# Idle transposes of the identity on TensorE, at five places of a decoder trunk's opening

## The chip, the cores and the metric

The kernel runs on one NeuronCore of a Trainium2 chip. The metric is the device time of one execution in microseconds; lower is better. The engines are TensorE (PE in the rows, its weight loads PEld), VectorE (DVE), ScalarE (ACT), GpSimd (POOL) and SyncE (SP), which issues most of the transfers.

## The reference

One inference step of a two-layer decoder trunk, in float32. A prompt of 512 tokens and 8 x 8 sample tokens go through the same weights: 576 tokens, model width 1024, feed-forward width 2816. Each layer is a half feed-forward, a mixer (a Conformer convolution in the first layer, dilated window attention in the second) and another half feed-forward. Cut to what matters here:

```python
def rmsnorm(x, g):
    xf = x.astype(jnp.float32)
    y = xf * lax.rsqrt(jnp.mean(xf * xf, axis=-1, keepdims=True) + EPS)
    return (y * g.astype(jnp.float32)).astype(x.dtype)

def swiglu_ffn(h, w_in, w_out):
    gate, up = jnp.split(h @ w_in, 2, axis=-1)
    return (jax.nn.silu(gate) * up) @ w_out

# for each layer li
x = x + 0.5 * swiglu_ffn(rmsnorm(x, norms[li, 0]), ffn_w_in[li, 0], ffn_w_out[li, 0])
...
```

The change touches only what runs ahead of and inside the first product of the first feed-forward.

## The kernel before

x is held transposed: model width on the partitions (eight tiles k of 128), tokens along the free side (576). x arrives in token order, in two halves of the columns (semaphores x_in0 and x_in1), as xr. TensorE turns each tile k with four transposes of 128 x 128 against the identity `ident` (L2361), and for every second k the 64 sample tokens of two tiles (L2369). Ahead of these it turns the six norm gains, loaded as rows of parR, with eight narrow transposes (L2349). ScalarE copies the turned tiles k = 0, 1, 2, 3, 6, 7 from PSUM to xT (L1209); VectorE copies 4 and 5 (L1762) and the sample parts (L1748).

A matmul of the feed-forward is not done as one product. Every float32 operand is split into a high part, cast by ScalarE to the type fp32r, and a low part, which VectorE gets by subtraction; a product is three matmuls, high by high, high by low, low by high (L2157 to L2159, 288 columns each). On top of this, the product of the first weight matrix with h is cut into 2 x 2 blocks (gate and up by the two halves of every pair of k tiles; the two halves of the tokens) and done with seven block products, P1 to P7, in place of eight. Their operands are sums of blocks:

- on the side of x, the terms: ScalarE multiplies xT by the gain (L1065, into hW and hM), VectorE forms sums (L1529 to L1535), ScalarE casts (L1071) and VectorE forms the low parts (L1542), into tE (for P1, P6, P5) and tM (for P2, P7, P3, P4). This is done for four pairs p of k tiles, one after the other;
- on the side of the weights: blk holds a unit's blocks as loaded (L614) and their sums (L1572, L1578, L1584). ScalarE casts (L1087) and VectorE forms the low parts (L1549), into hlA (A1 for P1, A2 for P2 and P4) and hlS (SA for P6 and P7, SB for P5 and P3).

The width 2816 is processed in two segments of eleven units of 128. `units` runs each unit's seven products, `outputs` the second weight matrix. The first unit of the first segment is `first_unit`: since its terms come out pair by pair, it runs the products' quarters by pair, P1, P6, P2, P7, P5 for p = 0, then for 1 and 2, then P4 and P3 for the three, then all seven for p = 3. Behind it stand two matmuls of the reciprocal norm's diagonal (L2258), then the second unit, which begins with P1 and needs its own A1.

Every engine has its own hand-written order and waits on semaphores: f_ready (weight parts), t_ready (terms), x_ready (tiles of xT), gain_ready (VectorE has copied the gains from PSUM bank 7). On ScalarE the order of the opening is: x tiles 0 and 1, the terms of pair 0, x tiles 2 and 3, casts of pair 0, x tiles 6 and 7, cast A1, the terms of pair 1, squares of x for the norm (L1197), cast SA, casts of pair 1, casts A2 and SB, and so on. On VectorE the order follows it.

Of the kernel before, what the change touches and what calls it, by code (L numbers as in the profile page):

```python
# [14 lines left out]
P = 128  # L15
# [111 lines left out]
def split_no(n, g, what, u):  # L127
    if n == g == u == 0 and what in FIRST_SPLITS:
        return FIRST_SPLITS.index(what) + 1
    return (SEGS * n + g) * len(SPLIT[g]) + SPLIT[g][what, u]  # L130
# [14 lines left out]
def term_no(n, p, x):  # L145


    base = 3 * (KD // 2) * n
    if n == 2:
        return base + (2 * p + x if x < 3 else KD + p + 1)  # L150
    return base + 3 * p + x
# [136 lines left out]
def trunk_program(nc, I, O):  # L288
# [3 lines left out]
    def place(name, shape, dt=f32):  # L292
        t = nc.alloc_sbuf_tensor_at(name, shape, dt, offset=at[0])
        at[0] += (int(np.prod(shape[1:])) * 4 + 31) // 32 * 32
        return t
# [10 lines left out]
    ident = place("ident", [P, P])  # L306
# [145 lines left out]
    ps = nc.alloc_psum_tensor("ps", [P, 8, 512], f32)  # L452
# [44 lines left out]
    S = {n: nc.alloc_semaphore(n) for n in names}  # L497
# [485 lines left out]
    def _(act):  # L983
# [391 lines left out]
        def keys_prompt(j, g):  # L1375

            q, _, _ = TURN["kp", j, g]
            act.wait_ge(S["t_mm"], q + 1)
            nc.scalar.copy(kT[:, j % 2, 4 * g:4 * g + 4, :].rearrange("p x n -> p (x n)"), turned(("kp", j, g))
                           ).then_inc(S["t_act"], 1)  # L1380

        def keys_sample(e, x, j):

            q, _, _ = TURN["ks", e, x, j]
            a = (C1, C2)[x]
            act.wait_ge(S["t_mm"], q + 1)
            nc.scalar.copy(kTs[:, j, a:a + 512], turned(("ks", e, x, j))).then_inc(S["t_act"], 1)
# [22 lines left out]
        for s in range(-1, UNITS + 3):  # L1410
            if 0 <= s - 1 < UNITS:
                exp(s - 1)
            ks = sample_keys_of(s)
            if ks and ks[1] < 2:
                for j in (0, 1, 3):
                    keys_sample(*ks, j)
            elif ks:
                keys_dense(ks[0])
            kp = prompt_keys_of(s)
            if kp:  # L1420
                keys_prompt(*kp)
            if 0 <= s - 2 < UNITS:
                q, _, _ = TURN["p", s - 2, 1]
                act.wait_ge(S["t_mm"], q + 1)
                nc.scalar.copy(pT[:, 4:8, :].rearrange("p x n -> p (x n)"), turned(("p", s - 2, 1))
                               ).then_inc(S["t_act"], 1)
# [669 lines left out]
    def _(pe):  # L2096
# [17 lines left out]
        def square_sum_tokens(bank=6):  # L2114
            t_ = tokens(tb)
            for t in range(TT):
                r = P if t < 4 else SMP
                nc.tensor.matmul(ps[0:r, bank, t:t + 1], t_[:, t * P:t * P + r], ones[:, 0:1], start=True, stop=True)
            return nc.tensor.matmul(ps[SMP:P, bank, 4:TT], t_[:, SEQ:TOK], ones[:, 0:1], start=True, stop=True)
# [32 lines left out]
        def quarter(what, p):  # L2152

            out = ps[:, P_BANK[what], 0:HALF]
            wh, wl = WEIGHTS[what]
            cols = slice(p * P, (p + 1) * P)
            nc.tensor.matmul(out, wh[:, cols], TERM[what][:, p, 0], start=p == 0, stop=False)  # L2157
            nc.tensor.matmul(out, wh[:, cols], TERM[what][:, p, 1], start=False, stop=False)  # L2158
            nx = nc.tensor.matmul(out, wl[:, cols], TERM[what][:, p, 0], start=False, stop=p == KD // 2 - 1)  # L2159
            if p == KD // 2 - 1:  # L2160
                nx.then_inc(S["f_mm"], 1)
# [6 lines left out]
        def parameters():  # L2168
            pe.wait_ge(S["par_in"], 16 * 9)
            for k in range(KD):  # L2170
                nx = nc.tensor.transpose(ps[:, 4, k * NPAR:(k + 1) * NPAR], parR[:, k * P:(k + 1) * P],
                                         ident[0:NPAR, 0:NPAR])
            nx.then_inc(S["par_t"], 1)

        def add_square(k):

            n, t = SQ["ffn3_in"] - 1, tokens((tb, ta)[k % 2])
            pe.wait_ge(S["sq_in"], KD * n + k + 1)
            for g, (a, b) in enumerate(((0, TOK - 2 * P), (2 * P, TOK))):
                nx = nc.tensor.matmul(ps[32 * g:32 * g + 32, 4, 0:b - a], ones[:, 0:32], t[:, a:b], start=k == 0,  # L2180
                                      stop=k == KD - 1, tile_position=(0, 32 * g))
            if k < KD - 2:
                nx.then_inc(S["sq_added"], 1)
            elif k == KD - 1:
                nx.then_inc(S["sq_ready"], 1)

        def turn_sums():

            a = HALF + SMP // 2
            pe.wait_ge(S["row_out"], 1)  # L2190
            for t in range(TT):
                g, c = divmod(t, 2) if t < 4 else (1, 2)
                rows, one = sum_rows[:, c * P:min(c * P + P, TOK - 2 * P)], ident[0:64, 32 * g:32 * g + 1]
                r = rows.shape[1]
                nc.tensor.matmul(ps[0:r, 4, a + t:a + t + 1], rows, one, start=True, stop=True)
            nx = nc.tensor.matmul(ps[SMP:P, 4, a + 4:a + 5], rows, one, start=True, stop=True)
            nx.then_inc(S["ss_done"], 1)

        def first_unit(n):

            x = KD * XV[f"ffn{n}_in"]

            def part(what, p):
                if p == 0:
                    pe.wait_ge(S["f_ready"], split_no(n, 0, {"P1": "A1", "P2": "A2", "P4": "A2", "P6": "SA", "P7": "SA",
                                                             "P5": "SB", "P3": "SB"}[what], 0))
                pe.wait_ge(S["t_ready"], term_no(n, p, {"P1": 1, "P5": 1, "P6": 2}.get(what, 3)))
                quarter(what, p)

            if n == 2:  # L2210

                for what in ("P1", "P6", "P5"):
                    if what == "P5":
                        pe.wait_ge(S["kv_evac"], 32)
                    for p in range(4):
                        part(what, p)
                pe.wait_ge(S["kv_evac"], 35)
                for p in range(4):
                    for what in ("P2", "P7", "P4", "P3"):
                        part(what, p)  # L2220
            else:
                if n == 0:
                    pe.wait_ge(S["x_ready"], KD)
                    pe.wait_ge(S["gain_ready"], 1)

                for p in range(3):
                    for what in ("P1", "P6", "P2"):
                        part(what, p)
                    if p == 0:
                        pe.wait_ge(S["x_ready"], x + KD - 1)  # L2230
                    for what in ("P7", "P5"):
                        part(what, p)
                if n == 3:
                    add_square(KD - 2)
                    add_square(KD - 1)
                elif n == 0:
                    parameters()
                pe.wait_ge(S["x_ready"], x + KD)
                if n == 1:
                    for p in range(3):  # L2240
                        part("P4", p)
                    pe.wait_ge(S["sq_ready"], SQ["ffn1_in"])
                    square_sum_tokens(4).then_inc(S["ss_done"], 1)
                    for p in range(3):
                        part("P3", p)
                else:
                    for p in range(3):
                        for what in ("P4", "P3"):
                            part(what, p)
                if n == 3:  # L2250
                    turn_sums()
                for what in FIRST[0]:
                    part(what, 3)

            pe.wait_ge(S["diag_ready"], n + 1)
            if n == 0:
                pe.wait_ge(S["par_ready"], 1)
            nc.tensor.matmul(ps[:, 4, :], ones[:], diag[:, 0:4].rearrange("p a b -> p (a b)"), start=True, stop=True  # L2258
                             ).then_inc(S["bc_mm"], 1)
# [84 lines left out]
        pe.wait_ge(S["ident_ready"], 1)  # L2344
        pe.wait_ge(S["consts_ready"], 1)

        pe.wait_ge(S["norms_in"], 16)
        for k in range(KD):
            nx = nc.tensor.transpose(ps[:, 7, k * 6:(k + 1) * 6], parR[NORM:NORM + 6, k * P:(k + 1) * P],  # L2349
                                     ident[0:6, 0:6])  # L2350
        nx.then_inc(S["gain_t"], 1)

        for k in range(KD):
            if k % 4 == 0:
# [489 lines left out]
```

## Time and profile before

| | us |
|---|---|
| median of 3 runs | 2262.54 |
| lowest and highest run | 2262.34, 2266.04 |
| the profiled execution | 2262.11 |
| its span, first to last instruction | 2260.2 |

| engine | busy us | share |
|---|---|---|
| TensorE, matmuls | 2214.9 | 98% |
| TensorE, weight loads | 2102.0 | 93% |
| VectorE | 1617.6 | 72% |
| ScalarE | 890.1 | 39% |
| GpSimd | 137.3 | 6% |

The span is cut on the page into 40 slices of 56.5 us, so the whole stretch that the change touches lies in the first. A timeline is needed for it: each of its rows gives the start, the length from the first start to the last end of the instructions that it merges, the engine, the line, what is written from what, and in brackets how long the engine sat idle before, and what let it go. A matmul's end is modelled, and matmuls overlap, so the spacing of starts says what one costs. The granted clock is 1.00 at 2.4 GHz and 0.50 at 1.2 GHz.

### The profile page before, as it was taken

What the parts mean: (1) busy time and instruction counts of PE and PEld (TensorE: products, weight loads), DVE (VectorE), ACT (ScalarE), POOL (GpSimd) and SP (SyncE); (2) the same over time, 40 slices, a digit from 0 to 9 for tenths busy, and PEclk for the clock granted to TensorE, in tenths of its full rate; (3) what the DMA queues carried; (4) which work ended last, traced back from release to release, by engine and by line L of the source; (5) the groups of instructions that cost most, each with busy time, mean ns of one, the idle gap of its engine ahead of it and who ended that gap; (6) DMA issues with size and microseconds to landing.
All of it is one profiled execution on the core that took longest, in us unless ns stands there. A gap on an engine that the chain in (4) does not pass through costs nothing.

```text
span 2260.2 us, 41620 instructions
## 1 busy us (share of the span) xinstructions
PE 2214.9 (98%) x17636; PEld 2102.0 (93%) x17636; DVE 1617.6 (72%) x2138; ACT 890.1 (39%) x1167; POOL 137.3 (6%) x191
## 2 busy tenths in 40 slices
PE   7999999999999999999999999999999999999998
PEld 6999999987799999998889999999987789999998
DVE  7983995699789849953358956984445479947963
ACT  6431443222654314432234422442145555413442
POOL 0000000323010000001001000001001100000001
PEclk8999999999899999999999999999999999999999
DMA  5543443554244435423439533532959933233321
GB/s 156 158 151 110 151 156 93 164 141 126 72 147 150 140 100 164 153 83 90 132 107 304 173 114 99 168 115 73 240 148 281 253 113 94 75 98 96 88 77 55
DMA packets 372091, 305.61 MB, mean 135 GB/s; under 512 B 13798, under 2 KB 338414, under 8 KB 371050
## 3 DMA queue, kind: packets, MB, share of 16 engines
q1 hardware_dynamic: 365485, 232.06, 36.4%
q0 software_dynamic: 6464, 71.76, 9.2%
q8 instruction: 86, 1.41, 0.3%
q14 instruction: 44, 0.35, 0.1%
q10 hardware_dynamic: 12, 0.02, 0.0%
HBM read 284.45 MB, written 70.54 MB: 157 GB/s over the span
## 4 chain that ended last, share of the span: by engine, by line
PE 88%; DVE 6%; issue 2%; ACT 2%; DMA 2%; SPq 1%; DVEq 0%; ACTq 0%
PE ps L2101 34%; PE ps L2157 13%; PE ps L2159 13%; PE ps L2158 13%; PE ps L2565 2%; PE ps L2563 2%; PE ps L2564 2%; PE ps L2401 2%; PE ps L2609 1%; DMA kc<-in_cache_kv_w 1%; DVE blk L1572 1%; PE ps L2725 1%; DVE hlS L1549 1%; PE ps L2663 1%; PE ps L2716 1%
## 5 line engine op out<-in xcount | busy, mean ns | idle before, releaser
L1087 ACT CAST hlS<-blk 128x1024 fp32r<-128x1024 f32 x176 | 184.3, 1053 | 207.0 <-PE ps L2159 169.4
L2101 PE MATMUL ps<-actH,oWA 128*128 128x288 f32 x1408 | 250.4, 296 | 0.0
L2101 PE MATMUL ps<-actH,oWB 128*128 128x288 f32 x1408 | 250.0, 296 | 0.0
L1716 DVE SCALAR_TENSOR_TENSOR cs<-ps,rstd 128x576 f32<-128x576 f32 x64 | 48.5, 757 | 246.9 <-PE ps L2101 246.9
L1549 DVE TENSOR_TENSOR hlS<-blk,hlS 128x1024 fp32r<-128x1024 f32 x176 | 213.5, 1216 | 2.4 <-ACT hlS L1087 2.4
L2157 PE MATMUL ps<-tM,hlA 128*128 128x288 f32 x704 | 212.4, 302 | 2.9 <-DVE hlA L1549 2.4
L2157 PE MATMUL ps<-tE,hlS 128*128 128x288 f32 x704 | 208.5, 296 | 4.1 <-DVE hlS L1549 4.1
L2101 PEld LDWEIGHTS ps<-actH,oWA 128*128 128x128 f32 x1408 | 209.0, 189 | 1.2 <-DVE cs L1611 0.6
L2101 PEld LDWEIGHTS ps<-actH,oWB 128*128 128x128 f32 x1408 | 209.0, 189 | 0.0
L2157 PE MATMUL ps<-tM,hlS 128*128 128x288 f32 x704 | 208.2, 296 | 0.0
L2158 PE MATMUL ps<-tM,hlA 128*128 128x288 f32 x704 | 208.0, 295 | 0.0
L2159 PE MATMUL ps<-tM,hlA 128*128 128x288 f32 x704 | 207.5, 295 | 0.0
L2158 PE MATMUL ps<-tE,hlS 128*128 128x288 f32 x704 | 207.5, 295 | 0.0
L2159 PE MATMUL ps<-tE,hlS 128*128 128x288 f32 x704 | 207.2, 294 | 0.0
L2158 PE MATMUL ps<-tM,hlS 128*128 128x288 f32 x704 | 207.2, 294 | 0.0
L2159 PE MATMUL ps<-tM,hlS 128*128 128x288 f32 x704 | 206.9, 294 | 0.0
L1488 DVE TENSOR_TENSOR wHL<-wst,wHL 128x1024 fp32r<-128x1024 f32 x64 | 82.2, 1285 | 116.8 <-ACT wHL L995 116.7
L1116 ACT ACTIVATE ta<-ta 128x576 f32<-128x576 f32 x88 | 60.5, 687 | 266.5 <-DVE ta L1631 266.5
L2101 PE MATMUL ps<-hH,wHL 128*128 128x288 f32 x896 | 158.5, 297 | 0.0
L1549 DVE TENSOR_TENSOR hlA<-blk,hlA 128x1536 fp32r<-128x1536 f32 (+2 forms) x104 | 156.0, 1504 | 0.9 <-ACT hlA L1087 0.9
L1087 ACT CAST hlA<-blk 128x1536 fp32r<-128x1536 f32 (+2 forms) x104 | 132.3, 1280 | 47.6 <-PE ps L2101 29.7
L2101 PE MATMUL ps<-actL,oWA 128*128 128x288 f32 x704 | 150.8, 296 | 0.0
(323 smaller groups left out, 5363.3 us busy)
## 6 DMA issues: line engine op xcount, KB each, us to landing
blk<-in_ffn_w_in SPq DMA_DIRECT2D x352, 256.0 KB, 4.1
raws<-in_ffn_w_out SPq DMA_DIRECT2D x64, 704.0 KB, 4.7
out_kv_sample<-in_cache_kv_w POOLq DMA_DIRECT2D x8, 4064.0 KB, 16.8
out_kv_sample<-in_cache_kv_w POOLq DMA_DIRECT2D x8, 2016.0 KB, 9.2
wst<-in_conv_w_pw SPq DMA_DIRECT2D x24, 512.0 KB, 4.1
wst<-in_w_kv SPq DMA_DIRECT2D x24, 512.0 KB, 3.8
kc<-in_cache_kv_w SPq DMA_DIRECT2D x40, 256.0 KB, 9.1
kc<-in_cache_kv_w SPq DMA_DIRECT2D x8, 1024.0 KB, 7.7
```

Source lines behind the costliest of these rows:

```text
L1087: nc.scalar.copy(o, a).then_inc(S["f_h"], 1)
L1116: nc.scalar.activation(ta[:], ta[:], ACT.Silu).then_inc(S["silu_done"], 1)
L1488: nc.vector.tensor_tensor(wL[:, s % 2, 0:size], wst[:, s, 0:size], wH[:, s % 2, 0:size].bitcast(f32), ALU.subtract).then_inc(S["w_ready"], 1)
L1549: nc.vector.tensor_tensor(o, a, h.bitcast(f32), ALU.subtract).then_inc(S["f_ready"], 1)
L1716: nc.vector.scalar_tensor_tensor(px[m % 2], pair(2 + m % 2), 0.5, rstd[:], ALU.mult, ALU.mult).then_inc(S["px_ready"], 1)
L2101: nx = nc.tensor.matmul(outs[t], a, b[:, t, :], start=start and first, stop=stop and b is xh and not first)
L2157: nc.tensor.matmul(out, wh[:, cols], TERM[what][:, p, 0], start=p == 0, stop=False)
L2158: nc.tensor.matmul(out, wh[:, cols], TERM[what][:, p, 1], start=False, stop=False)
L2159: nx = nc.tensor.matmul(out, wl[:, cols], TERM[what][:, p, 0], start=False, stop=p == KD // 2 - 1)
L2401: nc.tensor.matmul(ps[32 * g:32 * g + 32, 0, :], dW[:, s, g, k, :], uV[:, s, g, 4 * k:4 * k + SEQ], start=k == 0, stop=k == NS - 1, tile_p ...
L2563: nc.tensor.matmul(ps[:, t, :], xh, a, start=k == 0, stop=False)
L2564: nc.tensor.matmul(ps[:, t, :], xh, b, start=False, stop=False)
```

## The change

A helper, `keep_busy(bank, times)`, issues so many transposes of the identity by the identity, 128 x 128, into a PSUM bank that nothing reads before it is written anew. No semaphore is raised by them. It is called at five points of TensorE's program: 4 before the wait for the norms, 14 behind the gains' transposes, 28 before the first product (where the wait for gain_ready is now taken ahead of them, and the one for x_ready behind), 30 behind P1 of the first pair and 16 behind its P6; 92 in all. Only the first feed-forward (n = 0) is touched.

```diff
@@ -2196,6 +2196,11 @@
             nx = nc.tensor.matmul(ps[SMP:P, 4, a + 4:a + 5], rows, one, start=True, stop=True)
             nx.then_inc(S["ss_done"], 1)
 
+        def keep_busy(bank, times):
+
+            for _ in range(times):
+                nc.tensor.transpose(ps[:, bank, 0:P], ident[:], ident[:])
+
         def first_unit(n):
 
             x = KD * XV[f"ffn{n}_in"]
@@ -2220,12 +2225,15 @@
                         part(what, p)
             else:
                 if n == 0:
+                    pe.wait_ge(S["gain_ready"], 1)
+                    keep_busy(7, 28)
                     pe.wait_ge(S["x_ready"], KD)
-                    pe.wait_ge(S["gain_ready"], 1)
 
                 for p in range(3):
                     for what in ("P1", "P6", "P2"):
                         part(what, p)
+                        if n == p == 0 and what != "P2":
+                            keep_busy(4, 30 if what == "P1" else 16)
                     if p == 0:
                         pe.wait_ge(S["x_ready"], x + KD - 1)
                     for what in ("P7", "P5"):
@@ -2344,11 +2352,13 @@
         pe.wait_ge(S["ident_ready"], 1)
         pe.wait_ge(S["consts_ready"], 1)
 
+        keep_busy(6, 4)
         pe.wait_ge(S["norms_in"], 16)
         for k in range(KD):
             nx = nc.tensor.transpose(ps[:, 7, k * 6:(k + 1) * 6], parR[NORM:NORM + 6, k * P:(k + 1) * P],
                                      ident[0:6, 0:6])
         nx.then_inc(S["gain_t"], 1)
+        keep_busy(6, 14)
 
         for k in range(KD):
             if k % 4 == 0:
```

What the order of TensorE's instructions is at the beginning of the program: `ident` is the identity, `parR` the gains' rows, `xr` x in token order. Before:

```order
L2349 MATMUL ps<-ident,parR 128x6 x8
L2361 MATMUL ps<-ident,xr 128x128 x8
L2369 MATMUL ps<-ident,xr 128x64 x2
L2361 MATMUL ps<-ident,xr 128x128 x8
L2369 MATMUL ps<-ident,xr 128x64 x2
```

And with the change:

```order
L2202 MATMUL ps<-ident 128x128 x4
L2358 MATMUL ps<-ident,parR 128x6 x8
L2202 MATMUL ps<-ident 128x128 x14
L2371 MATMUL ps<-ident,xr 128x128 x8
L2379 MATMUL ps<-ident,xr 128x64 x2
L2371 MATMUL ps<-ident,xr 128x128 x8
```

Four idle transposes stand ahead of the gains' and fourteen between them and x; the rest keeps its order.

The same engine from the last tiles of x to P2 of the first pair, where tE and tM are the terms, hlA and hlS the weights. Before:

```order
L2361 MATMUL ps<-ident,xr 128x128 x8
L2369 MATMUL ps<-ident,xr 128x64 x2
L2157 MATMUL ps<-tE,hlA 128x288
L2158 MATMUL ps<-tE,hlA 128x288
L2159 MATMUL ps<-tE,hlA 128x288
L2157 MATMUL ps<-tE,hlS 128x288
L2158 MATMUL ps<-tE,hlS 128x288
L2159 MATMUL ps<-tE,hlS 128x288
L2157 MATMUL ps<-tM,hlA 128x288
```

And with the change:

```order
L2371 MATMUL ps<-ident,xr 128x128 x8
L2379 MATMUL ps<-ident,xr 128x64 x2
L2202 MATMUL ps<-ident 128x128 x28
L2157 MATMUL ps<-tE,hlA 128x288
L2158 MATMUL ps<-tE,hlA 128x288
L2159 MATMUL ps<-tE,hlA 128x288
L2202 MATMUL ps<-ident 128x128 x30
L2157 MATMUL ps<-tE,hlS 128x288
L2158 MATMUL ps<-tE,hlS 128x288
L2159 MATMUL ps<-tE,hlS 128x288
L2202 MATMUL ps<-ident 128x128 x16
L2157 MATMUL ps<-tM,hlA 128x288
```

Twenty-eight stand ahead of P1, thirty between P1 and P6, sixteen between P6 and P2. The orders of the other engines are the same before and after.

## Rows read from the trace of the kernel before

**Rows 1.** The page: span, and granted clock in 40 slices, in tenths.
```profile
span 2260.2 us, 41620 instructions
...
PEclk8999999999899999999999999999999999999999
```

**Rows 2.** Stretches (us): length, TensorE busy (matmuls), clock, DMA share, GB/s.
```profile
17.00:18.00 1.00, 0.36 (x1) 0.60 0.73 159
18.00:26.00 8.00, 1.79 (x6) 0.50 0.46 119
80.00:100.00 20.00, 20.00 (x152) 1.00 0.85 279
```

**Rows 3.** TensorE's timeline: start us, length us, line, operands, count, [idle before].
```profile
2.78 0.99 PE L2349 MATMUL ps<-ident,parR 6*128 6x6 f32 x8 [2.78 <-DMA parR<-in_norms]
6.91 1.97 PE L2361 MATMUL ps<-ident,xr 128*128 128x128 f32 x8 [3.14 <-DMA xr<-in_x_sample]
...
9.21 1.64 PE L2361 MATMUL ps<-ident,xr 128*128 128x128 f32 x8
...
11.04 1.09 PE L2361 MATMUL ps<-ident,xr 128*128 128x128 f32 x8
...
13.54 0.33 PE L2369 MATMUL ps<-ident,xr 64*128 64x64 f32 x2
17.64 0.58 PE L2157 MATMUL ps<-tE,hlA 128*128 128x288 f32 x1 [3.77 <-DVE hlA L1549]
...
22.83 0.61 PE L2157 MATMUL ps<-tE,hlS 128*128 128x288 f32 x1 [4.13 <-DVE hlS L1549]
...
26.27 0.61 PE L2157 MATMUL ps<-tM,hlA 128*128 128x288 f32 x1 [2.36 <-DVE hlA L1549]
...
30.76 0.34 PE L2157 MATMUL ps<-tM,hlS 128*128 128x288 f32 x1
...
40.82 0.40 PE L2157 MATMUL ps<-tE,hlA 128*128 128x288 f32 x1 [0.20 <-DVE hlA L1549]
```

**Rows 4.** Weight loads in 9.2 to 10 and 11 to 12: busy us, mean ns.
```profile
L2361 PEld LDWEIGHTS ps<-ident,xr 128*128 128x128 f32 x5 | 0.9, 218 | 0.1
...
L2361 PEld LDWEIGHTS ps<-ident,xr 128*128 128x128 f32 x8 | 0.9, 140 | 0.1
```

**Rows 5.** Timeline of the other engines, up to the first weight cast.
```profile
1.19 0.29 POOL L863 TENSOR_SCALAR_AFFINE_SELECT ident<-ident 128x128 f32<-128x128 f32 x1 [0.25 <-POOL ident L861]
...
8.06 0.58 ACT L1209 COPY xT<-ps 128x512 f32<-128x512 f32 x1 [5.20 <-PE ps L2361]
...
8.91 0.58 ACT L1209 COPY xT<-ps 128x512 f32<-128x512 f32 x1 [0.27 <-PE ps L2361]
...
9.63 0.29 DVE L1748 COPY xT<-ps 128x128 f32<-128x128 f32 x1 [5.62 <-ACT xT L1209]
10.02 0.78 ACT L1065 ACTIVATE hW<-xT,par 128x576 f32<-128x576 f32 x1 [0.53 <-DVE xT L1748]
...
15.23 0.64 ACT L1087 CAST hlA<-blk 128x512 fp32r<-128x512 f32 x1
```

**Rows 6.** The chain of waits: start us, length us, who.
```profile
16.79 0.60 DVE hlA L1549
...
40.09 0.68 DVE hlA L1549
```

**Rows 7.** TensorE's waits, 60 to 100 us: total, times, longest.
```profile
PE ps L2157 <- DVE hlA L1549: 0.9, 1, 0.9
```

**Rows 8.** x_sample's two transfers; the first unit's last two weight transfers: issue, landing.
```profile
L583 SPq DMA_DIRECT2D xr<-in_x_sample x2: 534/562/590, 1.3 to 2.5; - x2
...
DMA to landing us min/median/max: 5.6/6.8/8.0
...
L614 SPq DMA_DIRECT2D blk<-in_ffn_w_in x2: 1400/1640/1881, 4.3 to 5.7; - x2
...
DMA to landing us min/median/max: 8.2/8.4/8.7
```

## The prediction

> **What bounds the kernel now.** I read the page first, then the granted clock by stretches, then TensorE's own timeline of the first 41 us, and last the chain of waits over the same stretch, because the change touches nothing behind the first part of the opening unit.
>
> The page's clock row has an 8 only in the first of 40 slices [rows 1]. The change acts on that slice. The stretches show the clock at half level (0.50, 1.2 GHz) from 18 to 26 us, having fallen within the microsecond before [rows 2]. TensorE's timeline shows why there was little work [rows 3]: its last transpose of x starts at 13.54, the first product P1 waits 3.77 us until 17.64, P6 waits 4.13 until 22.83, and P2 waits 2.36 until 26.27. After that it runs without a wait, at first at 0.24 us a matmul (19 of them from 26.27 to 30.76 [rows 3]); at the full clock, from 80 to 100 us, 152 matmuls fill 20.00 us, 0.13 each [rows 2]. So 25 matmuls ran slowly, six of them in the first two products.
>
> There is a second slow piece, which the clock column doesn't show, since it reads 1.00 from the start. The first eight transposes of x took 1.97 us, the next eight 1.64, and eight of the same shape from 11.04 on 1.09 [rows 3]; weight loads of one shape fell from 218 to 140 ns in the mean [rows 4]. With the modelled end of one taken off (0.43 and 0.28 us), the spacing is (1.97 - 0.43)/7 = 0.22 and (1.09 - 0.28)/7 = 0.116 us, a factor of about two. I read this as half level at 6.91 and full level from some 10.2 on, and nothing but transposes ran between.
>
> Which of the two pieces sets the end? The chain of waits does not go through TensorE between 9 and 41 us. It leaves it after the first transposes of x (ScalarE copies at 8.06 and 8.91, VectorE's copy at 9.63, ScalarE's gain multiply at 10.02 [rows 5]) and then runs on VectorE and ScalarE alone, through the first hlA at 16.79, up to the hlA of the next unit at 40.09 [rows 6]. TensorE starts the next unit at 40.82, 0.20 us behind its own last work, let go by that hlA [rows 3]. It waits once more for 0.9 us between 60 and 100 us [rows 7], and the chain passes to it there. So what TensorE does faster between 17 and 40 us is absorbed at 40.82; what the first two groups of x do faster goes through.
>
> **The change part by part.** Base: the profiled execution took 2262.1 us, of which the span is 2260.2 and 1.9 lie around it; the median of the runs is 2262.5. I forecast differences and put them on the median.
>
> (1) Four transposes before the norms arrive. The identity is finished at 1.19 + 0.29 = 1.48 [rows 5]. At the slow spacing, 4 x 0.22 = 0.9 us, so the slot is free at about 2.5, before the norms' transposes at 2.78. Cost 0.
>
> (2) Fourteen more before x. The norms' eight transposes start at 2.78 and take 0.99 with the last one's end. 14 x 0.22 = 3.1 us from 3.6 ends at 6.7, just under the 6.91 at which x is there. Cost 0; if the first starts 0.3 later, 0.1 to 0.2 us. VectorE's copy of the gains depends only on what is ahead of these fourteen.
>
> (3) The transposes of x at full speed. The clock rose, before, some 3.4 us behind the start of the x transposes, and at 30.8, 4.6 us after the unbroken run began at 26.27 [rows 3]. Now TensorE works, almost unbroken, from 2.78. The two bounds put the rise at 6.2 to 7.4, where the transposes of x begin. At full speed the fourth transpose ends at 6.91 + 3 x 0.116 + 0.28 = 7.54 and the eighth at 8.00, against 8.0 and 8.88. ScalarE's first copy moves from 8.06 to 7.6; the second follows it on its engine at 8.15 instead of 8.91, since now ScalarE and not TensorE is late. VectorE's copy at 9.63 and all that hangs on it move by the same 0.76 us. The bounds for this term are 0 (the clock rises no sooner than before) and 0.8; I take 0.7. What could eat it next? The second half of x is all issued by 2.51 and lands within 8.0 us, thus by 10.5 [rows 8]; its transposes start at 11.04 before and can start at 10.5, soon enough for VectorE, which asks for them around 12. The last of the opening unit's four weight transfers lands at about 5.7 + 8.2 = 13.9 [rows 8]; the cast that needs it stands at 15.23 and would move to 14.5 [rows 5]. Neither takes the gain.
>
> (4) Twenty-eight before P1. They start when the last x tile is turned, 13.9 before and about 13.1 now: 28 x 0.116 = 3.25 us, end by 16.4, ready for P1 at 17.64 - 0.76 = 16.9. Cover about 0.5 us. Cost 0.
>
> (5) Thirty before P6: from about 17.3, 30 x 0.116 = 3.5, end 20.8 to 21.1, needed at 22.83 - 0.76 = 22.1. Cover 1.0 us, cost 0. Sixteen before P2: from 22.5, 16 x 0.116 = 1.9, end 24.4 to 24.7, needed at 25.5. Cost 0. No other queue is passed: the other engines' orders are unchanged.
>
> (6) The opening products at full speed. The gaps left are about 1 us, against 3.8 and 4.1, so the clock stays up. 25 matmuls x (0.24 - 0.13) = 2.7 us less TensorE work. TensorE then catches up with VectorE's terms of the third and fourth pair and waits for them. Its next unit still starts when VectorE has hlA. Value at the end: 0 by the chain, 2.7 as the far bound.
>
> Sum: 0 + 0 - 0.7 + 0 + 0 + 0 = -0.7 us, so 2262.5 - 0.7 = 2261.8.
>
> The row that the sum leans on is that transposes alone brought the clock up [rows 3, 4]. The Trainium skill, in "TensorE: Matmul & The Clock Gate", section "Part 4: PE-mode transpose", states the opposite: the full clock does not engage for transpose mode, since it doesn't count as TensorE being busy in the same way. By that rule the change would give the slower rival below; the trace of this case speaks against it.
>
> **Rivals.**
> *Slower: idle transposes at half level.* If the idle transposes don't raise or hold the clock, each block runs at 0.22. 28 x 0.22 = 6.2 from 13.9 puts P1 at about 20.1. 30 x 0.22 = 6.6 behind P1's 0.7 puts P6 at 27.4, and 16 x 0.22 = 3.5 behind its 0.7 puts P2 at 31.6, against 26.27. That is 5.3 us later, less the 0.2 of wait at 40.82: +5.1, so 2267.6. It decides in the gap between P1 and P6: from 18.5 to 22.83 are 4.3 us, so thirty transposes begin to cost above 0.145 us each. For it: the 0.22 of the first group. Against it: the same form at 0.116 from 11.04 on.
> *No gain.* The clock rises no earlier than 10.2, or the fourteen run into x by as much as they give. Then 2262.5. For it: cover is only 0.2 us before 6.91, and two rises are all that the trace has.
> *TensorE's gain counts.* If the chain is misread and TensorE is the bound by 40 us, the 2.7 us of (6) come on top: 2262.5 - 0.7 - 2.7 = 2259.1. Against it: the wait of 0.20 for hlA at 40.82 and 0.9 later [rows 3, 7]; each would only grow.
>
> **How the numbers follow.** Forecast 0.74, no gain 0.13, TensorE's gain counts 0.08, slower 0.05. A measurement of this kernel can tell about 0.2%, 4.5 us: faster is below 2258.0, slower above 2267.0. The forecast, no gain, and nearly all of the third lie within. Faster gets 0.02 from the third with some of the runs' spread, slower 0.04 from the slower rival, the same 0.94. The range goes from 2259.0, which takes in the third rival, to 2265.0: no gain, and part of the spread that the three runs of before show (2262.3 to 2266.0). The slower rival stays outside.
>
> **What would show it.** Right: the first eight transposes of x take about 1.1 us, not 2.0; ScalarE's second copy starts near 8.2 and VectorE's copy near 8.9; the idle blocks run at about 0.12 each and the clock column has no 0.50 between 13 and 34 us; P1, P6 and P2 start near 16.9, 22.1 and 25.5, let go by VectorE; TensorE shows new waits for VectorE's terms between 28 and 37; the next unit starts near 40.1, again let go by hlA. Wrong: idle blocks at 0.22, P6 or P2 later than 22.83 or 26.27, or an unchanged second copy at 8.9. A start of the next unit much before 40 would speak for the third rival. If all of this holds and the total is still off by over 1 us, something far behind the opening moved, which no row here foretells.

## The result, and the profile after

| | before | after |
|---|---|---|
| median, us (22 runs each) | 2264.61 | 2268.68 |
| lowest to highest, us | 2260.50 to 2266.47 | 2264.37 to 2272.09 |
| profiled execution, us | 2262.1 | 2265.9 |
| its span, us | 2260.2 | 2264.0 |

The ratio of after to before is 1.0020, 95% interval 1.0014 to 1.0026: about 4.1 us slower. The forecast was 0.7 us faster, and its range ended at 2265.0. Of the kernel late74 below, two of eleven executions took over 3070 us and are left out of its median.

The page of after first. It answers to rows 1.

```profile
span 2264.0 us, 41803 instructions
...
PE 2224.8 (98%) x17728; PEld 2111.0 (93%) x17728; DVE 1616.4 (71%) x2138; ACT 890.6 (39%) x1167; POOL 138.1 (6%) x191
...
PEclk9999999999899999999999999999999999999999
...
q8 instruction: 87, 1.43, 0.3%
```

The 8 of the first slice has become a 9. The instruction count rose from 41620 to 41803, by 183. That number decides this case: 92 transposes are 92 weight loads and 92 matmuls, less one wait that is no longer an instruction of its own. The queue q8, which the page lists as of the kind "instruction", shows 87 transfers (86 before).

TensorE's timeline of the first 41 us, in the columns of rows 3:

```profile
1.53 1.11 PE L2202 MATMUL ps<-ident 128*128 128x128 f32 x4 [1.53 <-POOL ident L863]
2.70 1.02 PE L2358 MATMUL ps<-ident,parR 6*128 6x6 f32 x8
3.65 3.25 PE L2202 MATMUL ps<-ident 128*128 128x128 f32 x14
6.88 1.20 PE L2371 MATMUL ps<-ident,xr 128*128 128x128 f32 x8
...
13.26 3.27 PE L2202 MATMUL ps<-ident 128*128 128x128 f32 x28
16.74 0.37 PE L2157 MATMUL ps<-tE,hlA 128*128 128x288 f32 x1 [0.20 <-issue]
...
17.21 3.44 PE L2202 MATMUL ps<-ident 128*128 128x128 f32 x30
22.08 0.40 PE L2157 MATMUL ps<-tE,hlS 128*128 128x288 f32 x1 [1.43 <-DVE hlS L1549]
...
25.52 0.40 PE L2157 MATMUL ps<-tM,hlA 128*128 128x288 f32 x1 [1.03 <-DVE hlA L1549]
...
30.91 0.40 PE L2157 MATMUL ps<-tM,hlA 128*128 128x288 f32 x1 [0.81 <-DVE tM L1542]
...
40.07 0.40 PE L2157 MATMUL ps<-tE,hlA 128*128 128x288 f32 x1 [0.47 <-DVE hlA L1549]
```

The opening did what the prediction said, almost row by row. The first eight transposes of x take 1.20 us, not 1.97. P1, P6 and P2 start at 16.74, 22.08 and 25.52. The next unit starts at 40.07, not 40.82, again let go by hlA. (In brackets, "issue" means that the engine waited for nothing that the profile can name; more of it below.)

The other engines, from the timeline of 5 to 12 us, answer to rows 5:

```profile
7.67 1.07 ACT L1209 COPY xT<-ps 128x512 f32<-128x512 f32 x2 [4.82 <-PE ps L2371]
8.88 0.29 DVE L1748 COPY xT<-ps 128x128 f32<-128x128 f32 x1 [4.92 <-ACT xT L1209]
9.27 0.78 ACT L1065 ACTIVATE hW<-xT,par 128x576 f32<-128x576 f32 x1 [0.53 <-DVE xT L1748]
```

VectorE's copy moved from 9.63 to 8.88 and ScalarE's gain multiply from 10.02 to 9.27, both by 0.75 us. The stretch in which the clock stood at 0.50 before reads 1.00 now (columns as in rows 2, with the busy time of each engine):

```profile
13.00:34.00 21.00, 17.44 (x138) 16.00 (x138) 19.33 (x32) 18.67 (x30) 0.00 (x0) 1.00 0.61 159
```

So the loss lies behind the opening. To find it, I took the same matmul in both traces, at many places, and subtracted the starts. After minus before is -0.76 us at 40, still -0.79 at 571, +1.96 at 595, +1.57 at 1667, +0.12 at 1700 and +3.71 at 1784, where it stays to the end. There are two steps up. (The drop ahead of 1700 is a dip of the granted clock that only before has in 1670 to 1680: 0.83 against 1.00.) Two stretches of TensorE show them (us, busy, clock, DMA share, GB/s), first before:

```profile
575.00:600.00 25.00, 22.22 (x146) 0.73 0.15 43
1700.00:1800.00 100.00, 93.42 (x1530) 0.98 1.06 285
```

and after:

```profile
575.00:600.00 25.00, 22.36 (x136) 0.66 0.15 43
1700.00:1800.00 100.00, 90.44 (x1471) 0.97 1.01 273
```

The first step, 2.75 us at 595, is a difference in where a dip of the granted clock falls: 0.73 against 0.66. It is not the change's, as the experiments show. The second, 3.6 us, lies in the attention, between 1700 and 1800 us, where the DMA share is over 1: the queues are full. TensorE's waits there, total, times and longest, before:

```profile
PE ps L2609 <- DMA kc<-in_cache_kv_w: 2.4, 2, 1.4
PE ps L2725 <- issue: 2.4, 1, 2.4
PE ps L2654 <- issue: 0.9, 1, 0.9
```

and after, where the lines of the code are numbered ten higher:

```profile
PE ps L2619 <- DMA kc<-in_cache_kv_w: 4.1, 2, 3.9
PE ps L2735 <- issue: 3.1, 1, 3.1
PE ps L2619 <- issue: 1.3, 1, 1.3
```

"issue" means that the engine waited for nothing that the profile can name: no semaphore was missing, and still it stood for 0.9 to 3.1 us. In the timeline before, these two places are

```profile
1737.99 0.63 PE L2654 MATMUL ps<-kT,qc 64*32 64x253 f32 x7 [0.91 <-issue]
...
1754.57 0.65 PE L2725 MATMUL ps<-rstd,pT 128*32 128x128 f32 x7 [2.37 <-issue]
```

and after

```profile
1714.99 0.38 PE L2619 MATMUL ps<-ident,kc 128*128 128x128 f32 x2 [1.34 <-issue]
...
1777.17 0.71 PE L2735 MATMUL ps<-vcA,pT 128*32 128x128 f32 x17 [3.13 <-issue]
```

The stops are in other places of the same code. TensorE has 511 instructions between the two stops of before, and 1792 between those of after: 2 x 256, less one, and 7 x 256. What could come every 256 instructions? The page says 1.43 MB in 87 transfers for q8, thus 16 KB each, and 16 KB over 256 instructions is 64 bytes for one. The counts agree: from 1700 to 1800 us of before the trace has 13 transfers of q8 and 3132 instructions of TensorE, 12.2 blocks. The DMA view of before, over the 3 us ahead of the stop at 1754.57, has one such transfer among the cache rows (queue, packets, MB, share of 16 engines):

```profile
q1 hardware_dynamic: 390, 0.71, 104.5%
q8 instruction: 1, 0.02, 2.5%
```

2.5% of 16 engines for 3.1 us is 1.2 us of one engine, among engines that the cache rows keep busy. I read the stops as TensorE at the end of what it had fetched, with the next block of 256 instructions behind cache rows in a DMA queue. How long such a request stood in the queue isn't in the trace; that it depends on the load is tested below with light queues.

### The profile page after: what moved, and what is told of

It is laid out like the page before. It is cut to its first block, busy times and chain, and to the rows that moved or that the text cites. A ratio compares the mean times of both kernels' runs of the same rounds, so it can differ in the third digit from the quotient of the medians.

```text
span 2264.0 us, 41803 instructions
## 1 busy us (share of the span) xinstructions
PE 2224.8 (98%) x17728; PEld 2111.0 (93%) x17728; DVE 1616.4 (71%) x2138; ACT 890.6 (39%) x1167; POOL 138.1 (6%) x191
## 3 DMA queue, kind: packets, MB, share of 16 engines
q8 instruction: 87, 1.43, 0.3%
## 4 chain that ended last, share of the span: by engine, by line
PE 87%; DVE 5%; DMA 3%; issue 2%; ACT 2%; SPq 1%; DVEq 0%; ACTq 0%
PE ps L2101 34%; PE ps L2157 13%; PE ps L2159 13%; PE ps L2158 13%; PE ps L2575 2%; PE ps L2573 2%; PE ps L2574 2%; PE ps L2411 2%; DMA blk<-in_ffn_w_in 1%; PE ps L2619 1%; DMA kc<-in_cache_kv_w 1%; DVE blk L1572 1%; PE ps L2735 1%; PE ps L2726 1%; DVE hlA L1549 1%
```

## Experiments: what TensorE does early, or how many instructions it has

**Theory A.** The 183 further instructions shift every later end of a block of 256. In the attention, where the queues are full, an end can cost a stop, and its price depends on where in the code it falls. Any 183 instructions would do that; 256 would do nothing.

**Theory B.** The idle transposes cost time by what they do: the opening runs 0.75 us earlier and at another clock, and later transfers, or the dips of the clock, fall worse.

For each kernel I measure the median, its ratio to runs of before on the same chip at the same time, and in its trace the stretch of the attention from the first scores (kTs, qs) to the seventh of the eight transposes of oSs, which took 138.5 us before (1672.05 to 1810.53).

**The same opening with 256 instructions more (pad256).** A narrow transpose is one of six columns. Five idle transposes ahead of P1 are left out, and 41 narrow ones stand in their places and behind the others, with two waits that are met anyway (one of them is an instruction of its own), so that TensorE's program is 256 instructions longer and all block ends behind the opening fall on the same instructions as before.

```diff
+        def narrow(bank, times):
+            for _ in range(times):
+                nc.tensor.transpose(ps[:, bank, 0:6], ident[0:6, 0:P], ident[0:6, 0:6])
...
-                    keep_busy(7, 28)
+                    keep_busy(7, 23)
+                    narrow(7, 15)
...
                             keep_busy(4, 30 if what == "P1" else 16)
+                            if what == "P1":
+                                pe.wait_ge(S["sums"], 2)
+                                pe.wait_ge(S["t_h"], 1)
+                            narrow(4, 14 if what == "P1" else 12)
```

> The changed kernel with 36 narrow idle transposes more (6 columns of the identity) and one satisfied wait more, in the same waits of the opening, five of the full idle ones taken out: TensorE's program is then 256 instructions longer than before, 256 x 64 bytes being the 16384 bytes of one instruction transfer in the trace, where the change made it 183 longer. Theory A (the shift of TensorE's instructions against the blocks in which they are fetched costs the time, by fetches that come late in the attention part, where the DMA engines are full): the boundaries are back at the places of before and the opening's 0.8 us stays: ratio to before 0.9997, time 0.5 to 1.5 us below before. Theory B (the 0.8 us head start or the idle work itself costs, by the clock or by transfers that meet otherwise): 3 to 5 us above before, as the changed kernel.

Measured: 2263.20 us, ratio 0.9997 (0.9988 to 1.0006); the stretch 135.3 us.

**183 instructions without the idle work (shift183).** The kernel before, with 92 narrow transposes in the gaps of the opening pair.

```diff
                 if n == 0:
-                    pe.wait_ge(S["x_ready"], KD)
                     pe.wait_ge(S["gain_ready"], 1)
+                    narrow(7, 26)
+                    pe.wait_ge(S["x_ready"], KD)
...
+                        if n == p == 0 and what != "P2":
+                            narrow(4, 46 if what == "P1" else 20)
```

> The kernel before with 92 narrow idle transposes (6 columns) behind the transposes of x only: the same 183 instructions more as in the change, but no head start, since nothing is ahead of x. Theory A: 4 to 5 us above before (ratio 1.002), with waits of TensorE for nothing but its instructions (releaser 'issue') at the places where the changed kernel has them, L2619 and L2735 there. Theory B: within 1 us of before.

Measured: 2266.69 us, ratio 1.0010 (1.0001 to 1.0019); the stretch 143.2 us. The 2.0 us lie between the two theories' figures, 4 to 5 and within 1.

**The three again (after2, pad256b, shift183b).** The interval of shift183 reached from nearly nothing to nearly the whole loss, so these repeat after, pad256 and shift183, unchanged, side by side.

> The changed kernel again, beside the three others of this call on one chip. Theory A: 3 to 5 us above before, and 4 to 6 above pad256b.

> The version of 256 instructions more again. Theory A: 0 to 1.5 us below before. If the first figure was chance, it lies between before and after2.

> The shift by 183 instructions alone, behind the transposes of x, again. It gave +2.0 us where the changed kernel has +4.1, with nothing ahead of x. Theory A alone: equal to after2 or up to 1 us above it. If the idle work has a price of its own as well, 1 to 3 us below after2.

Measured:

| kernel | instructions more | median, us | ratio (95%) | attention stretch, us |
|---|---|---|---|---|
| after2 | 183 | 2268.70 | 1.0022 (1.0013 to 1.0031) | 143.5 |
| shift183b | 183 | 2268.33 | 1.0021 (1.0012 to 1.0030) | 143.7 |
| pad256b | 256 | 2264.87 | 1.0002 (0.9993 to 1.0011) | 138.6 |

This decides between the theories. Narrow transposes, with nothing of the early clock, cost what the change costs. The change's opening with a whole block more costs nothing that the runs can tell from zero (pad256b was expected up to 1.5 us below before, and lies 0.6 above). The stops say the same. TensorE's timeline between 1700 and 1800 us of after2, its rows with such an idle:

```profile
1716.54 0.38 PE L2619 MATMUL ps<-ident,kc 128*128 128x128 f32 x2 [1.46 <-issue]
...
1778.65 0.82 PE L2735 MATMUL ps<-vcA,pT 128*32 128x128 f32 x17 [2.61 <-issue]
...
1797.68 2.05 PE L2735 MATMUL ps<-vcB,pT 128*32 128x128 f32 x66 [0.77 <-issue]
```

of shift183b:

```profile
1715.29 0.38 PE L2617 MATMUL ps<-ident,kc 128*128 128x128 f32 x2 [1.62 <-issue]
...
1733.55 1.30 PE L2733 MATMUL ps<-vcA,pT 128*32 128x128 f32 x40 [0.46 <-issue]
...
1777.93 1.04 PE L2733 MATMUL ps<-vcA,pT 128*32 128x128 f32 x17 [2.51 <-issue]
...
1796.40 2.05 PE L2733 MATMUL ps<-vcB,pT 128*32 128x128 f32 x66 [0.22 <-issue]
```

and of pad256b:

```profile
1739.97 0.63 PE L2674 MATMUL ps<-kT,qc 64*32 64x253 f32 x7 [1.21 <-issue]
...
1757.32 0.42 PE L2745 MATMUL ps<-rstd,pT 128*32 128x128 f32 x7 [3.15 <-issue]
```

The two kernels with 183 stop where after stops, at the same operands with the same counts behind (kc x2, vcA x17). The kernel with 256 stops where before stops, at kT,qc x7 and rstd,pT x7. A stop costs 0.2 to 3.2 us, and the same place isn't always equally dear (2.37 before, 3.15 in pad256b), as it would if it depends on what is in the queue.

**Where in a block the stops fall.** The block's end can be located in every trace, not only by the distance of two stops. I count all of TensorE's instructions (weight loads, matmuls and the sequencer's own) from the first of the trace, which is 0. In the twelve traces with full queues there are 34 idles put down to "issue" of over 0.15 us in the attention. All 34 end at an instruction whose number leaves 243 or 244 when divided by 256, whatever was inserted. Each ends 1.2 to 1.8 us behind the end of a transfer of q8, so a late block is what TensorE had waited for. Outside the attention the only such idles stand before P1 (0.20 us in after, at a remainder of 193): they are of another kind.

The sum of the stops alone doesn't give the loss. Over the stretch the traces have, in us:

| | before | pad256b | after2 | shift183b |
|---|---|---|---|---|
| stretch | 138.5 | 138.6 | 143.5 | 143.7 |
| "issue" | 3.3 | 4.4 | 4.8 | 4.8 |
| waits for kc | 2.4 | 1.8 | 3.0 | 3.2 |
| clock at 0.50 | 6.8 | 6.4 | 13.5 | 13.7 |

The last row weighs most. The clock from 1700 to 1800 us was 0.98 in before (above). The same row of after2:

```profile
1700.00:1800.00 100.00, 91.31 (x1477) 0.95 0.99 275
```

of shift183b:

```profile
1700.00:1800.00 100.00, 91.34 (x1458) 0.95 0.99 269
```

and of pad256b:

```profile
1700.00:1800.00 100.00, 92.92 (x1529) 0.98 1.05 287
```

At 0.50 the engine does about half of what it does at 1.00 (0.24 against 0.13 us a product's matmul in the prediction's rows). By that estimate 6.7 us more of it are some 3.3 of the 5.0 us that after2 is longer than before, the stops 1.6 and the waits for kc 0.6. Together these are 5.5, thus 0.5 too much. With 183 instructions more, a block ends at 1715 in the transposes of kc themselves (ident,kc), and the longest wait for kc, the next sample's key rows, is 3.0 to 4.0 us in the four runs, against 1.4 to 1.8 in before, pad256 and pad256b. That the stops also bring the later kc and the dips of the clock was not tried apart. Several dips begin within 0.5 us of the end of a stop (1754.58 in before, 1779.11 in after2, 1778.15 in shift183b), and with light queues, below, stops, waits for kc and dips are all gone from 1700 to 1800 us; but shift73 and early18 have 7.7 and 6.0 us of stops and a clock of 1.00 there.

**One part alone (early18, late74).** early18 has only the eighteen idle transposes ahead of x (36 instructions), late74 only the seventy-four around P1 and P6 (147).

```diff
+        keep_busy(6, 4)
         pe.wait_ge(S["norms_in"], 16)
...
         nx.then_inc(S["gain_t"], 1)
+        keep_busy(6, 14)
```

> The first 18 idle transposes alone (4 and 14): the whole head start of 0.8 us, and 36 instructions more. Theory A: an own figure for another shift, somewhere from 1 below to 5 above before; the fetch waits stand at other instructions than in both kernels. Theory B by the head start: 3 to 5 us above before. The opening in both: next unit's P1 at about 40.1.

> The last 74 idle transposes alone (28, 30 and 16): no head start, clock kept up between 17 and 31 us, 147 instructions more. Theory A: an own figure for this shift, from 0 to 5 us above before, with fetch waits at other instructions. Theory B by the head start: within 1 us of before. The next unit's P1 at about 40.8, as before, in both.

Measured: early18 2266.74 us, 1.0010 (1.0001 to 1.0019), stretch 142.2; late74 2269.43 us, 1.0020 (1.0011 to 1.0030), stretch 143.3. Theory B by the head start had 3 to 5 us for the first, which took 2.1, and under 1 for the second, which took 4.8. Neither part is innocent, and both together cost no more than late74 alone. A cost by what each part does would add up; one by position needn't. early18 stops at instructions 768, 511 and 1281 apart, late74 at 1279, 256 and 256: multiples of 256 again, to within one.

early18 has a second use. Its first transposes of x, which come behind eighteen idle ones as in after:

```profile
6.71 1.95 PE L2368 MATMUL ps<-ident,xr 128*128 128x128 f32 x8
...
8.91 1.09 PE L2368 MATMUL ps<-ident,xr 128*128 128x128 f32 x8
```

The first eight still run at half the speed, as in rows 3, and the next eight at full. So the clock rose at some 8.7 us here and at some 7.1 in after, with the same work ahead of it. Term (3) of the sum has its size in after by luck of that moment.

**Other shifts (pad220, shift73).** pad220 is after with eighteen narrow transposes and two waits more, shift73 is early18 with nineteen idle transposes ahead of P1.

```diff
                             keep_busy(4, 30 if what == "P1" else 16)
+                            if what == "P1":
+                                pe.wait_ge(S["sums"], 2)
+                                pe.wait_ge(S["t_h"], 1)
+                            narrow(4, 10 if what == "P1" else 8)
```

> The changed kernel with 37 instructions more in the opening's waits, 220 in all. Theory A: the damage is a function of the shift alone, by which instruction a block ends on; 220 is another point of it (36 gave +2.1 us, 147 +5.6, 183 +4.1, 256 -1.5 against before). It names no value ahead, only that the fetch waits stand some 18 matmuls earlier than with the 256, and that the time is between -1.5 and +6. Theory B (head start or idle work): 3 to 5 us above before.

> The first 18 idle transposes and 19 of the 28 ahead of P1, none behind P1 or P6: 73 instructions more. Another point of the shift; the head start is in, the clock falls after P1 as before. Theory A names only a range, -1 to +6 us. Theory B (head start or idle work): the head start's share of the 4 us, thus 3 to 5 if it is the head start, under 2 if it is the idle work's amount.

Measured: pad220 2264.91 us, 1.0001 (0.9992 to 1.0010), stretch 138.1; shift73 2266.71 us, 1.0013 (1.0004 to 1.0022), stretch 141.1. pad220 does more than after does, and is faster. shift73's 2.5 us lie between the two figures that theory B had for it (3 to 5, or under 2).

**The shift mended just ahead of the attention (latepad).** after, with 36 narrow transposes (72 instructions) ahead of the first sample unit: 183 more up to there, 255 in the attention.

```diff
                 e = sample_unit(i)
+                if e == 0:
+                    for _ in range(36):
+                        nc.tensor.transpose(ps[:, 0, 0:6], ident[0:6, 0:P], ident[0:6, 0:6])
+                    pe.wait_ge(S["k_in"], 48)
```

> The changed kernel as it is, with 72 narrow idle instructions more (36 transposes of 6 columns) in TensorE's wait of 2.2 us ahead of the first sample unit's scores, at the start of the attention. With the 183 of the change that makes 255, one short of a block of 256, for all that stands behind. Theory A, with the place of the damage in the attention part: the opening and the stretch to 1670 us are those of the changed kernel (0.8 us ahead until 570, then some 1 to 2 behind by the clock), the fetch waits in the attention stand where they stand before (L2654 and L2725 there), and the time is near before: 0.9990 to 1.0005 of it. If the damage came from before the attention, it stays: 3 to 5 us above before.

Measured: 2266.29 us, 1.0008 (0.9999 to 1.0017); stretch 137.7, with stops at 1742.02 (kT,qc x7) and 1758.83 (rstd,pT x6), the places of before. The attention is as short as before. Of the 2.1 us that are left in the median, the padding itself took 1.3, since it stands on TensorE's path: the scores start that much later against the work ahead of them. The other 0.8 is within the interval, and open. The ratio lies just above the 1.0005 that theory A allowed.

**The attention with light queues (lightbefore, lightafter).** before and after, with only 64 of the 512 columns loaded of the cache rows of most samples (keys from the second sample on, values from the third on). The attention computes with what the buffers held before; all else is as it was.

```diff
+            n = AW if b == 0 else 64
             if x == 0:
-                sp.dma_start(kc[:, 0:4, :], c512[b, :, :, 0, :]).then_inc(S["kc_in0"], 16)
+                sp.dma_start(kc[:, 0:4, 0:n], c512[b, :, :, 0, 0:n]).then_inc(S["kc_in0"], 16)
...
+            n = AW if b < 2 else 64
```

> The kernel before, with the cache transfers of the attention cut: from the second sequence of the keys and the third of the values on, only 64 of 512 columns are loaded, so the samples' attention is computed from old columns. TensorE's program is unchanged; the transfers of 1700 to 1800 us carry much fewer bytes. Theory A (a fetch is late because its transfer stands behind full queues): the waits for 'issue' (0.9 and 2.4 us before) fall below 0.3 us each, and those for kc go too; some 4 to 6 us below before. If the fetch waits are a fixed price of a block, they stay.

> The changed kernel with the same cut of the cache transfers: only 64 of 512 columns from the second sequence of the keys and the third of the values on. Theory A: with the queues empty the shift of 183 instructions costs nothing, and the time is 0.3 to 1.5 us below that of the kernel before with this cut. Theory B (the cost comes by the head start or the idle work, not by the fetches): it stays 3 to 5 us above that.

Measured: 2256.11 us (0.9961, 0.9947 to 0.9974) and 2256.45 us (0.9968, 0.9956 to 0.9980). The stretch took 130.0 and 130.2 us. These are five and six executions. The same 183 instructions now cost 0.3 us in the median and 0.2 in the stretch. Theory A had expected less of the cut (4 to 6 us, not 8) and lightafter 0.3 to 1.5 us below lightbefore, by the gain of the opening; in its trace the clock rose late and that gain was missing. TensorE's row of lightbefore between 1700 and 1800 us:

```profile
1700.00:1800.00 100.00, 98.83 (x1653) 1.00 0.29 73
```

and the only waits that lightafter has there:

```profile
PE ps L2692 <- DVE kTs L2001: 1.0, 3, 0.3
```

The DMA share fell from 1.06 to 0.29, and with it "issue" and the wait for kc are gone, in both. The ends of blocks are still in the program; with free queues they cost nothing. Where TensorE reaches the numbers with remainder 244, between 1700 and 1800 us, the last transfer of q8 had ended 2.4 to 8.2 us before.

All in one view, by what has been added ahead of the attention:

| kernel | instructions more | modulo 256 | median less before of its call, us | stretch, us | "issue" in 1700 to 1800, us |
|---|---|---|---|---|---|
| before | 0 | 0 | 0 | 138.5 | 3.3 |
| pad256, pad256b | 256 | 0 | -1.5, +0.6 | 135.3, 138.6 | 2.8, 4.4 |
| latepad | 255 | 255 | +2.1 | 137.7 | 3.4 |
| pad220 | 220 | 220 | +0.7 | 138.1 | 2.6 |
| early18 | 36 | 36 | +2.1 | 142.2 | 6.0 |
| shift73 | 73 | 73 | +2.5 | 141.1 | 7.7 |
| late74 | 147 | 147 | +4.8 | 143.3 | 6.0 |
| shift183, shift183b | 183 | 183 | +2.0, +4.1 | 143.2, 143.7 | 4.0, 4.8 |
| after, after2 | 183 | 183 | +4.1, +4.4 | 140.4, 143.5 | 4.5, 4.8 |

The second step of the traces, at 1700 to 1800 us, is thus the change's. The first, at 575 to 600, is not: lightbefore, which is before up to the attention, lies 2.9 us behind before at 595. Its row:

```profile
575.00:600.00 25.00, 22.34 (x130) 0.66 0.15 43
```

It has the clock of after with the instructions of before. Most of the fourteen traces show 0.66 here, shift73 and latepad 0.59, before 0.73 and shift183b, with after's 183 instructions, 0.80. So the profiled execution of before was a quick one here, and its time lies 2.5 us below the median of its kernel.

## Why the prediction was wrong

**(1), (2): right in the profile.** Four transposes at 1.53 and fourteen at 3.65 cost nothing. They ended at 6.9, where x was there; the row at 6.88 has no idle before it, so no cover was left. In after2, pad256b and lightafter the norms came 0.4 to 0.6 us later, and the fourteen held x back by 0.2 to 0.4 us, as "No gain" feared.

**(3): right in the profile, too sure as a mean.** The chain moved by 0.76 us, as the forecast said. But the clock doesn't rise at the same moment in each execution. In the nine profiles with the early idle transposes, the next unit's start moved by -1.06 to +0.15 us, -0.4 in the mean; in those without by -0.19 to +0.17. Part of this is only when x itself begins. From the first transpose of x to the next unit, before takes 33.92 us; five of the nine take 33.1 to 33.2, the whole gain, and the four in which the clock came late (early18, shift73, latepad, lightafter) 33.8 to 33.9. The term of 0.7 should have been some 0.4.

**(4), (5): right in their times.** 28 took 3.27 us (3.25 said), 30 took 3.44 (3.5). P1, P6 and P2 were 16.9, 22.1 and 25.5 in the forecast. In front of P6 and P2 TensorE still waited 1.43 and 1.03 for VectorE; before P1 the row says 0.20 of "issue" where the forecast had VectorE.

**(6): right.** TensorE caught up, waited 0.81 for tM at 30.91, and the next unit was let go by hlA. Nothing of the 2.7 us reached the end.

**The sum: a term was missing.** The failing sentence is in (5): "No other queue is passed: the other engines' orders are unchanged." The instructions themselves are carried by a queue, q8, and every one behind the opening was moved in it by 183. The missing term is the measured +4.1 less the -0.4 of (3), thus 4.5 us; in the traces of after2 and shift183b the attention stretch is 5.0 and 5.2 us longer than in before. The prediction's last paragraph left the place for it ("something far behind the opening moved"), but gave it neither a price nor a chance, while two rows pointed at it. The page of before has q8, and the waits of before have 3.3 us of "issue" where the DMA share is 1.06. They stood there as a cost that could belong to a position, though a size for another position could not be had from them.

**The rivals.** The slower one came nearest in its number (2267.6) and had the wrong reason: the idle transposes of the three later blocks ran at 0.11 us each, not 0.22 (the fourteen ahead of x did take 0.22), and P6 and P2 came earlier, not later. "TensorE's gain counts" is refuted by 40.07. "No gain" holds in four of the nine profiles, or nearly, for the reason that it names: a clock that comes late.

**The range.** It was made from the opening's terms alone, and could hold no loss from another stage. Its base was also 2.1 us low: the median of 22 runs of before is 2264.61, that of the three at hand was 2262.54.

## What to carry to other kernels

Work "for nothing" in an idle gap has a price that isn't in the gap: it lengthens the engine's program. Where another stage of the same engine shows idle put down to "issue", beside a DMA share near or above 1, any edit ahead of it that changes the number of instructions, a useful one too, moves those stops and can win or lose some microseconds (here -1.5 to +4.8 of 2264). Before an opening edit of that size is believed or discarded, pad the program to the next multiple of 256 instructions and measure again. Better still is to take load off the queues there: with a share of 0.29 the stops went, and 183 instructions more cost 0.3 us.

## What the runs showed of the hardware

**Instruction blocks.** TensorE stopped at distances of 511, 512, 768, 1279, 1281 and 1792 instructions, multiples of 256 to within one, for 0.2 to 3.2 us, only where the DMA share was about 1. Counted from the program's start, all 34 stops of the twelve traces ended at a remainder of 243 or 244, 1.2 to 1.8 us behind the end of a transfer of q8, each of which is of 16 KB. The Trainium skill, in "Runtime: NRT & Kernel Launch", section "Instruction fetch mechanics", gives such blocks, of 16 KiB and 256 instructions, and the traces agree. It calls the cost of crossing from one to the next mostly hidden; that held at a share of 0.29 (no "issue" row in the attention) and did not at 1.06.

**The clock with transposes alone.** Idle transposes of 128 columns raised the clock and held it: 28 in 3.27 us, 0.11 each, and 1.00 from 13 to 34 us. From 13.3 to 24.3 us TensorE ran 74 of them and six products. The Trainium skill's "TensorE: Matmul & The Clock Gate", section "Part 4: PE-mode transpose", says that transpose mode doesn't engage the full clock. The traces of this case contradict it, in both kernels, if these instructions use that mode: the profile lists them as MATMUL and doesn't tell.

**The clock's own moment.** With the same eighteen idle transposes, the first eight of x took 1.20 us in after and 1.95 in early18. In the nine profiles with them the trace's records of the clock put the rise at 6.6 to 9.7 us, against 10.1 to 15.2 in the five without. Work put in to raise the clock by a given time raised it at times that differ by 3 us between executions.
